# Decode attention: keys turned in 32x32 blocks by VectorE, scores as eight 32x64 row tiles of TensorE

## The reference

```python
scores = (einsum("bqhc,btc->bhqt", q_lat, ckv)      # 256 latent values a key
          + einsum("bqhr,btr->bhqt", q_rope, kr)) * MLA_SCALE   # 32 rotary values a key
p = softmax(where(k_pos <= q_pos, scores, NEG_INF))
o = einsum("bhqt,btc->bqhc", p, ckv)                # the latents are also the values
```

## Time and profile before

| | |
|---|---|
| median of 3 runs | 1533.65 us |
| profiled execution, own time | 1538.29 us |
| its span, first to last instruction | 1536.5 us |
| PE busy in the span | 1495.1 us, 97% |
| decode attention in the trace | from 434.8 to 686.6 us |
| last scores of the stage | 664.7 us |

### The profile page before, as it was taken

The page is one execution under the profiler, slowest core; times in us unless marked ns, Lnnn a source line. Parts: engine busy times, 40 slices in busy tenths (PEclk is TensorE's granted clock), DMA queues, the critical chain, the costliest instruction groups (busy, mean ns, idle before and its releaser), DMA issues.

```text
span 1536.5 us, 25744 instructions
## 1 busy us (share of the span) xinstructions
PE 1495.1 (97%) x9880; PEld 1325.9 (86%) x9880; DVE 667.3 (43%) x1454; ACT 437.9 (29%) x1050; POOL 390.3 (25%) x286
## 2 busy tenths in 40 slices
PE   7999999999989999989999999999999999999997
PEld 7998977775567777767999999999999999999885
DVE  3251367763533333334544352115633364019655
ACT  3322466661544444423111111111211121114100
POOL 3110067672023222102222222222222222226000
PEclk9999999999999999999999999999999999999999
DMA  5351020002644559474121111111211111113321
GB/s 210 123 217 33 1 83 1 1 1 76 187 120 122 159 159 232 141 274 138 49 49 42 42 49 48 48 43 36 55 43 47 42 46 46 42 42 110 111 85 66
DMA packets 104670, 131.24 MB, mean 85 GB/s; under 512 B 12354, under 2 KB 75650, under 8 KB 104548
## 3 DMA queue, kind: packets, MB, share of 16 engines
q1 hardware_dynamic: 102500, 125.39, 27.4%
q0 software_dynamic: 2048, 4.20, 1.1%
HBM read 113.84 MB, written 15.71 MB: 84 GB/s over the span
## 4 chain that ended last, share of the span: by engine, by line
PE 53%; DVE 0%; issue 0%; ACT 0%
PE ps L1986 46%; PE ps L2020 6%; PE ps L2006 1%; DVE p_h L2259 0%; DVE p_h L2256 0%; DVE p_stats L2242 0%; DVE p_h L2239 0%; PE ps L1997 0%; ACT p_rt L2066 0%; DVE p_mv L2245 0%; DVE p_rs L2249 0%; DVE p_ve L2247 0%
## 5 line engine op out<-in xcount | busy, mean ns | idle before, releaser
L1986 PE MATMUL ps<-p_xh,p_wh 128*128 128x352 f32 (+1 forms) x1152 | 377.0, 327 | 2.3 <-PEq L1701 2.3
L1986 PE MATMUL ps<-p_xl,p_wh 128*128 128x352 f32 (+1 forms) x1152 | 377.0, 327 | 0.0
L1986 PE MATMUL ps<-p_xh,p_wl 128*128 128x352 f32 (+1 forms) x1152 | 377.0, 327 | 0.0
L2074 POOL TENSOR_TENSOR p_wl<-p_wr,p_wh 128x512 fp32r<-128x512 f32 x116 | 162.9, 1420 | 517.5 <-DVE p_wh L2092 517.5
L1986 PEld LDWEIGHTS ps<-p_xh,p_wh 128*128 128x128 f32 x1152 | 216.7, 188 | 2.5 <-issue 2.5
L1986 PEld LDWEIGHTS ps<-p_xh,p_wl 128*128 128x128 f32 x1152 | 216.8, 188 | 0.0
L1986 PEld LDWEIGHTS ps<-p_xl,p_wh 128*128 128x128 f32 x1152 | 216.7, 188 | 0.0
L2092 DVE CAST p_wh<-p_wr 128x512 fp32r<-128x512 f32 x116 | 46.3, 433 | 338.7 <-ACT p_stage L2059 248.7
L2059 ACT ACTIVATE p_stage<-ps 128x384 f32<-128x384 f32 x168 | 79.4, 473 | 368.9 <-PE ps L1986 368.9
L904 POOL TENSOR_SCALAR p_pr<-p_pr,p_rec 128x896 f32<-128x896 f32 (+3 forms) x64 | 109.6, 1722 | 141.7 <-DVE p_rec L868 141.6
L945 POOL DMA_INDIRECT p_rawr<-cache_kr,p_rows x64 | 64.8, 1013 | 217.1 <-PE ps L1303 160.2
(11 more groups left out here) (311 smaller groups left out, 2643.8 us busy)
## 6 DMA issues: line engine op xcount, KB each, us to landing
p_rawc<-cache_ckv SPq DMA_DIRECT2D x256, 128.0 KB
p_wr<-w_in SPq DMA_DIRECT2D x104, 256.0 KB
x_kept<-p_xh SPq DMA_DIRECT2D x8, 544.0 KB
x_kept<-p_xl SPq DMA_DIRECT2D x8, 544.0 KB
p_xh<-x_kept SPq DMA_DIRECT2D x8, 544.0 KB, 4.2
p_xl<-x_kept SPq DMA_DIRECT2D x8, 544.0 KB, 7.2
p_xs<-x_prompt SPq DMA_DIRECT2D x8, 512.0 KB
p_wr<-w_o SPq DMA_DIRECT2D x16, 256.0 KB
```

The costliest lines, as they stand in the source:

```text
L1986: last = pe.matmul(ps[:, g % 8, 0:tn], w[:, v % HL, kt % UK, :], x[:, kt, t0:t0 + tn], start=(kt == 0 and q == 0), stop=(kt == nk - 1 and ...
L2074: nc.gpsimd.tensor_tensor(wl[:, v % HL], wr[:, v % RAW], f32(wh[:, v % HL]), ALU.subtract).then_inc(wl_done, 1)
```

## The change

- VectorE turns the keys straight from the page buffers in 32x32 blocks: `keys(n)`, two instructions of 128x1024 for the latents of two groups and one of 128x256 for their rotary parts. TensorE's transposes of keys, ScalarE's copies to `p_kT` and VectorE's to `p_rT` go away.
- After a block transpose a strip of 32 partitions holds 32 of the latent dimensions of the keys of one page. So the scores of a step are 8 products over 32 latent dimensions and one rotary product, each for 4 strips (row tiles) and 2 halves (column tiles): 72 matmuls of K=32, 64 query rows and 128 keys, with each strip in a PSUM bank of its own (banks 0 to 3). Both groups of a step stand in the same four banks, and there is one set of them.
- The queries must stand on every strip. `cross_prompt` stores them to DRAM (8 DMAs of 32x8x64, runs of 256 bytes) and SP loads them back four times for each sequence (`load_queries`), two sequences ahead of the stage and the others between page loads. `p_qlat` and `p_qrope` are laid out by sequence, and the copies of queries by VectorE (L1466, L1469) go.
- ScalarE now copies the probabilities to `p_pt` (VectorE only in the tail). The two halves of the outputs are normalised together and summed by TensorE against a doubled identity (`pair_id`); ScalarE's `p_olow` copy and VectorE's addition go.

```diff
-            def turn(n):
-                s = n % NAT
-                pe.wait_ge(raw_in[s], 64 * (n // NAT + 1))
-                for t in range(CT):
-                    u = CT * n + t
-                    if u >= 3:
-                        pe.wait_ge(kt_done, u - 2)
-                    for j in range(4):
-                        last = pe.transpose(ps[:, u % 3, j * P:(j + 1) * P], raw_c[:, s, j, t * P:(t + 1) * P],
-                                            k["ident"][:, :])
-                    last.then_inc(turned, 1)
...
             def scores(n):
-                b, g = n // G, n % G
-                it, q = item(b, g), b % 2
-                bank = 4 + it % 2
...
+                b, new = n // G, n % G == G - 2
+                x = n % 4
+                pe.wait_ge(q_in[b % 2], 64 * (b // 2 + 1))
+                pe.wait_ge(s_done, item(b, n % G))
+                pe.wait_ge(keys_done, n // 2 + 1)
+                cols = lambda i, f: ps[f * R:(f + 1) * R, i, 0:P].rearrange("p (x w a) -> p x a w", x=2, a=2)
+                for d in range(NB):
+                    for f in range(2):
+                        for i in range(4):
+                            rows = slice(32 * i, 32 * (i + 1))
+                            pe.matmul(cols(i, f), q_rows[rows, b % 2, d, :], kT[rows, x:x + 2, 2 * f:2 * f + 2, d, :],
+                                      start=(d == 0), stop=False, tile_position=(32 * i, f * R))
...
+            def keys(n):
+
+                for x in (n, n + 1):
+                    s = x % NAT
+                    dve.wait_ge(raw_in[s], 64 * (x // NAT + 1))
+                    if n >= 4 and x == n:
+                        dve.wait_ge(scored, n // 2 - 1)
+                    dve.transpose(kT[:, x % 4].rearrange("p a d w -> p (a d w)"), raw_c[:, s].rearrange("p a c -> p (a c)"))
...
+            sp.wait_ge(lat_kept, 1)
+            for t in range(CT):
+                for z in range(4):
+                    sp.dma_start(k["q_kept"][:, :, 4 * t + z, :].rearrange("b r w -> r b w"),
+                                 qlat[32 * z:32 * (z + 1), t, :, :]).then_inc(q_stored, 16)
             for n in range(PRE):
                 load_pages(sp, a, e, regs, n)
+            sp.wait_ge(q_stored, 16 * 4 * CT)
+            for b in range(2):
+                load_queries(sp, k, e, b)
...
             for n in range(0, NG, 2):
-                b, g = n // G, n % G
                 p = n - LAG
-                if n in side_of:
-                    side(n)
-                if p >= 0:
-                    probs(p)
-                    if p % G == 4:
-                        total(p // G)
-                for x in (n, n + 1):
-                    if x < NG:
-                        keep_scores(x)
-                if g == 4 and b + 1 < DECB:
-                    queries(b + 1)
-                if p >= 0 and p % G == G - 2:
-                    finish(p // G)
+                keep_scores(n)
+                keep_scores(n + 1)
+                if n + 4 < NG:
+                    keys(n + 4)
+                if p >= 0 and p % G == 4:
+                    total(p // G)
```

More of the change, by code:

```diff
@@ L1231, in decode_attention @@
     TAIL = NG - LAG
+    SIDE = 4
     def probs_at(p):
-        return (1, pt_tail) if p > TAIL and p // 2 % 2 == (TAIL // 2 + 1) % 2 else (6, pt)
+        return (5, pt_tail) if p > TAIL and p // 2 % 2 == (TAIL // 2 + 1) % 2 else (6, pt)
     def acc(b):
@@ L1321, in scores @@
-                bank = 4 + it % 2
-                pe.wait_ge(q_ready, b + 1)
-                if it >= 2:
-                    pe.wait_ge(s_done, it - 1)
-                for t in range(CT):
-                    u = CT * n + t
-                    pe.wait_ge(kt_done, u + 1)
-                    for e in range(2):
-                        pe.matmul(ps[e * R:(e + 1) * R, bank, 0:HK], qc[:, q, t, :], kT[:, u % 8, e * HK:(e + 1) * HK],
-                                  start=(t == 0), stop=False)
@@ new lines, in scores @@
+                for f in range(2):
+                    for i in range(4):
+                        rows = slice(32 * i, 32 * (i + 1))
+                        last = pe.matmul(cols(i, f), qrope[rows, b, :], rT[rows, x:x + 2, 2 * f:2 * f + 2, :],
+                                         start=False, stop=not (new and i == 0 and f == 0),
+                                         tile_position=(32 * i, f * R))
+                if new:
+                    o = ps[0:R, 0, P:P + NS]
+                    for t in range(CT):
+                        pe.matmul(o, qlat[:, t, b, :], k["cnT"][:, t, :], start=False, stop=False)
+                    last = pe.matmul(o, qrope[0:ROPE, b, :], k["krT"][:, :], start=False, stop=True)
@@ L1431, in exps, with finish @@
                                      accum_out=tots[0:r, b % 2, g + 1:g + 2]).then_inc(exped, 1)
-            copies(0)
-            copies(1)
-            for n in STEPS:
-                b, g = n // G, n % G
-                for x in (n + 2, n + 3):
-                    if x < NG:
-                        copies(x)
-                if G <= n < NG:
+            def finish(b):
+                act.wait_ge(pv_done, (b + 1) * G)
+                act.wait_ge(recd, b + 1)
+                nc.scalar.activation(on[:, :], ps[:, acc(b), 0:KVL], ACT.Copy,
+                                     scale=rec[:, b % 2:b % 2 + 1]).then_inc(o_normed, 1)
+            for n in range(0, NG, 2):
+                b, g = n // G, n % G
+                p = n - LAG
+                if p >= 0:
+                    if p % G == 0:
+                        side(p // G)
+                    probs(p)
+                if b:
                     if g == 0:
@@ L1457, in _ @@
+            for g in range(-1, G):
+                exps(DECB - 1, g)
         @block.vector
         def _(dve):
[L1459 to L1470 removed]
@@ L1563, in _, with place_out @@
+            def place_out(b):
+                dve.wait_ge(o_turned, b - DECB + 3)
+                for to, src in out_cols(b):
+                    last = dve.tensor_copy(to, src)
+                last.then_inc(o_placed, 1)
+            keys(0)
             dve.memset(zero[:, :], 0.0)
-            dve.memset(qr[:, :, :, :], 0.0)
+            dve.tensor_copy(pair_id[0:R, :], k["ident"][0:R, 0:R])
+            dve.tensor_copy(pair_id[R:P, :], k["ident"][R:P, R:P])
             dve.memset(tots[:, :, :], 0.0).then_inc(cleared, 1)
```

246 lines of the change are left out of this document (104 added, 142 removed).

## The result

| | before | after |
|---|---|---|
| median of runs beside each other | 1533.74 us | 1520.49 us (4 runs, 1519.35 to 1521.55) |
| ratio, 95% interval | | 0.9915, 0.9902 to 0.9927 |
| profiled execution, own time; span | 1538.29; 1536.5 us | 1519.35; 1517.6 us |
| first and last scores in the trace | 664.7 (last) | 443.2 and 644.8 |

What follows compares the result with a forecast made beforehand. TensorE's instruction stream was taken to bound the decode stage. Start 443.1, five steps of 3.75, maximum 1.1, clock 3, 27 steps of 4.95 and loads 8 gave last scores at 607.6, hence 1478 us median, range 1466 to 1490.

Steps and rivals of the forecast that it cites:

- Scores: Decode stage, TensorE: a step's 144 score records run in all eight tiles together, 1.96 us a step.
- Rival A: Scores: strips don't run together, 7.8 us a step for scores, steps of 10.8 us, 1650 us in all; chance 0.13.
- B: Scores: issue or weight loads go one by one, 27 ns a record, 3.9 us a step; 1526 to 1538 us; chance 0.18.
- A full step: Decode stage, TensorE: probabilities 0.6, scores 1.96, values 1.94 and a change of array shape 0.15, together 4.65 us.
- The boundary: Between sequences in the decode stage: 1.2 us on four steps, 0.3 each, making a step 4.95 us.
- Block transposes: VectorE's key turning: 1.1 us per 1024 columns, 2.5 us a step with the rotary one, hidden behind TensorE.
- Queries and barrier: SP's query stores and loads in cross_prompt put the barrier 5 us later, at 439.8; scores begin at 443.1.
- Loads: Decode stage: SP's page issues and the DMA engines fall behind, costing 8 us together (0 to 25).
- Clock: Start of the decode stage: TensorE's pause and idle first five steps lower its granted clock, costing 3 us.
- The tail: After the last scores: the same work as before, plus 1.5 us for what the DMA engines carry over.
- 27 steps of 4.95 us: Decode stage after its first five steps: 27 steps at 4.95 us each, taking the sum from 466 to 599.6.
- the 1517 us worked out with 25 ns a start: Alternative estimate for scores from the Trainium skill's 25 ns between starts: 3.6 us a step, 1517 us in all.

Runs made afterwards that it cites:

- the kernel with half out: The changed kernel without the second column half (f = 1) of latent blocks 1 to 7: 1497.32 us (0.9771 of before); repeated, 1513.82 us (0.9841).
- sets 3 and 4: Later groups of runs on two chips, repeating the unchanged changed kernel: 1557.45 us (1.0134 of the kernel before), then 1556.70 us (1.0124).
- set 4: Last group, on another chip: unchanged changed kernel 1556.70 us, with queries by GpSimd 1551.56, with 256 columns a matmul 1527.32, the kernel before 1537.98.
- set 1: First group of follow-up runs: kernel before 1532.26 us, changed kernel with queries by GpSimd 1516.66; the unchanged changed kernel wasn't run in it.

## Why the prediction was wrong, by its own steps

- *Scores.* Right. Eight tiles run together: 2.25 us where the line isn't interrupted (2.12 with fewer instructions), against 1.96. Rival A is out, and B as it stood too (records 27 ns apart, 3.9 us a step). Where the Trainium skill ("TensorE: Matmul & The Clock Gate", "Wait — 56ns, not 53.3ns?") has starts never under about 25 ns apart, the trace has 144 in 2.25 us, 16 ns: that doesn't hold across tiles.
- *A full step.* 4.65 forecast; 2.12 + 1.88 + 0.67 = 4.67 measured from the kernel with half out.
- *The boundary.* Mis-sized. 0.3 us on each step, 1.2 a sequence, was forecast. The boundaries of the kernel with half out stand 20.98 us apart (507.18 and 528.16 are the starts of L1315), so 20.98 - 4 x 4.67 = 2.3 us. In it are a wait of PE for `p_on` each time (0.40 us; 0.65 between the starts of L1306 and L1315), four records of L1315 where there were two, and two of L1366. 7 x 1.1 = 8 us.
- *Block transposes.* 1.22 us and 0.40 against 1.1 and 0.3. Covered, as forecast. The next rows are from 443.2 to 645.1.

```profile
L1470 DVE STREAM_TRANSPOSE p_kT<-p_rawc 128x1024 f32<-128x1024 f32 x62 | 73.4, 1222 | 0.3
...
L1474 DVE STREAM_TRANSPOSE p_rT<-p_rawr 128x256 f32<-128x256 f32 x31 | 12.5, 402 | 0.0
```

- *Queries and barrier.* Forecast 439.8 for the stage's begin and 443.1 for the scores; 439.83 and 443.23.
- *Loads.* Mis-sized. 8 us were forecast. In the changed kernel PE has no wait of its own for a page or a query: it stood still for other reasons. In the kernel with half out they show. PE waits 2.5 us for `p_on` at 551, 3.3 for queries at 574 and 5.85 for `p_on` at 585, and the granted clock is 0.84 from 560 to 590. Two sequences together last 17.7 us longer than the usual 21.0 (the same kernel's starts of L1342 stand 18.1, 21.0, 21.0, 21.0, 26.1, 33.6 and 21.0 apart; one pause named issue, 1.1 us, is in it). The mechanism was SP and DMA, as said, but the chain went through VectorE's order of work, which I had not followed.
- *Clock.* +3 us was forecast for the first steps. Low clock came later too: 0.88 from 560 to 590 in the changed kernel. No run measures its cost alone.
- *The tail.* +1.5 forecast, +0.9.
- **The step that failed** is "27 steps of 4.95 us", in what it takes for granted: that a step lasts as long as its work on the array. TensorE's records went from 9880 to 12904, all of the increase in this stage, and the sum gave an instruction no price beyond its start. I had asked whether *issue* would hold (rival B) and looked for its mark in the distance of starts; it was a mark in the number of instruction packets that was to be looked for, 18 in the stage before and then 1.25 a step. What the runs showed in its place: 24.1 us of PE's pauses in the score lines L1330 and L1335, 26.2 in all, 22.9 of them at every 256th instruction; taking 112 instructions a step away brought some 22 to 23 us at the same work for the array.

The 37 us by which the last scores were late: 23.8 go with half of the column half out, measured from the first to the last scores (201.6 against 177.8 us). The 13.3 that are left are, in that kernel, 8 for boundaries, some 10 for loads beyond the 8 forecast, and 5 the other way, at the stage's start and end; 1.9 of these 5 are a slip of the sum, which counts the last step's values ahead of the last scores. Some of the 23.8 is lower clock after long pauses (windows at 0.88 and 0.94), which isn't parted from them.

The forecast's sign was right with the chance at 0.72, on the first measurement. In sets 3 and 4 the same kernel is slower than the one before, by what the prediction had nothing for. That the 1517 us worked out with 25 ns a start lie so near the 1520.49 measured is chance: the scores lasted 2.25 us where they weren't interrupted, and not 3.6.

**A version that beats both.** 256 columns a matmul with the queries on GpSimd is 0.7% faster than before (0.9931) and 1.9% faster than the changed kernel in set 4, with every output computed. In set 1's conditions it was never run; there the best that computes everything was the changed kernel with its queries on GpSimd, 0.9894.

## What to carry to other kernels

Small matmuls in many tiles cost the array little, but each is a matmul and a weight load that have to be brought in. Count a stage's instructions for each microsecond of work beside its columns, and look at the "instruction" queue of the DMA view: when its packets in a stage go from one in 13 us to one in 5, look for pauses named "issue". Check them: here they came 256 records apart or a multiple of it, each just after a packet. Then make each instruction longer (more moving columns) before making more of them; with 256 columns in place of 128 those pauses were gone here. And where an in-order engine takes over work that waits for DMA, list what else it owes to others behind that wait.

## What the runs showed of the hardware

- Four row tiles by two column tiles of f32 matmuls run together: 144 records of 128 columns in 2.25 us.
- TensorE's instructions come in packets of 16 KB, 256 instructions. In the changed kernel, with one needed every 5.05 us on average, and 288 instructions of the scores used up in 2.25 us, it stood still for 0.4 to 3.2 us at a time, with data ready, and went on 1.3 to 1.7 us after a packet had landed. When page traffic fell from 0.73 to 0.28 of the DMA engines the pauses named issue fell from 26.2 to 14.9 us.
- After such a pause TensorE can find itself at the lower of its two clocks: L1369's matmuls, 16 of them in 1.95 us otherwise, started 0.42 us apart in pairs in place of 0.21 from 572.5 to 575.0 in the changed kernel, at the lower one (window as in the earlier trace rows):

```profile
572.50:575.00 2.50, 2.50 (x14) 1.42 (x12) 2.50 (x3) 0.00 (x0) 0.00 (x0) 0.50 1.03 292
```

- A block transpose of 128x1024 f32 from SBUF to SBUF takes VectorE 1.22 us, 1.2 ns a column.
- TensorE, and with it GpSimd and SyncE but not ScalarE, can halt every 0.74 us for stretches, in some sets of runs and not in others on the same chip. With that a kernel changed sign against another: 0.9915 in one set, 1.0134 in another. A comparison of kernels with unlike instruction counts should be repeated in a set of its own.
